# Modulation rows from raw fp32 weights instead of hi and lo halves

## The chip, the cores and the metric

The kernel runs on one core of a Trainium2 chip. The time is that of one execution on the device in microseconds; the figure compared is the median of several runs. The core has a matrix engine (TensorE, PE in the profile; its weight loads are PEld), a vector engine (VectorE, DVE), a scalar engine (ScalarE, ACT), GpSimd (POOL) and SyncE (SP), which here issues the transfers of weights.

## What is computed

The reference is a chain of two networks. The first has two layers whose norms are modulated by a condition vector; the second has two layers without it. The modulation is what matters here: the condition goes through silu and one wide matrix product, and gives shifts, scales and gates for the norms of both layers.

```
def modulate(x, shift, scale):
    return rms_norm(x) * (1.0 + scale) + shift
```

There are two condition vectors of 1024 numbers, for context and latent tokens. For two layers, six chunks and 1024 numbers each that makes 12288 outputs per condition from a 1024 x 12288 weight: 48 tiles of 1 MB, each giving 256 outputs.

## The kernel before, in words

All weights come as 436 tiles of 128 partitions x 2048 fp32 numbers through a ring of four buffers called raw. SyncE issues tile n+4 once TensorE has used tile n. For each tile ScalarE casts raw to fp32r (w_hi, two buffers, `split_hi`, L911), VectorE subtracts to get the rest (w_lo, written over raw, `split_lo`, L1178), and TensorE multiplies with both. A tile is thus a chain of landing, cast, subtraction, matmuls, and its w_hi buffer is free for the tile after next once the matmuls are done.

The order of the work is written out by hand for each engine, with counting semaphores: raw_full (landed), hi_done, lo_done, tile_used, sums_taken (the result was copied out of PSUM).

The first 48 tiles are the modulation. Per tile:
- `ada_rows`: 16 matmuls on TensorE, 8 blocks of 128 input numbers, each with w_hi (L476) and w_lo (L477) as the moving operand of 256 columns, and four stationary columns (the hi and lo parts of two conditions, tile cond). They give 4 x 256 in PSUM.
- `ada_copy` on VectorE (L1264) copies that to ada_row.
- `ada_turn`, one tile later, on TensorE (L484): two small fp32 matmuls put the 256 outputs on partitions, and add hi and lo parts by the 4 x 2 table parts_sum.
- `ada_add` on VectorE (L1268) adds the bias and writes mod.

Beside this ScalarE and GpSimd make tables of decays (L999, L330, L332). After the 48 tiles VectorE adds 1 to the scales (L1286), and the norm begins: ScalarE squares X (L937, after loading a table), TensorE sums the squares by fp32 matmuls of 512 columns with a table of ones (L465), and the product of the first stage (L366 to L368) follows. It needs tiles 48 and 49 split.

Of the kernel before, what the change touches and what calls it, by code (L numbers as in the profile page):

```python
# [26 lines left out]
F32R = mybir.dt.float32r  # L27
ALU = mybir.AluOpType
ACT = mybir.ActivationFunctionType
AX = mybir.AxisListType.X  # L30

P = 128
D = 1024
DC = D // P
T = 256
# [4 lines left out]
RET_H, RET_VB = 4, 4  # L40
# [6 lines left out]
RAW, SPLIT = 4, 2  # L47


ADA_TILES = 48  # L50
# [33 lines left out]
def build(nc, ws, xt, col1, row1, col2, row2, relb, cst, ret_cst, ret_dist, c64, out):  # L84
# [3 lines left out]
    def at(name, shape, kb, dtype=F32):  # L88
        return nc.alloc_sbuf_tensor_at(name, shape, dtype, offset=base + int(kb * KB) // 32 * 32)


    raw = at("raw", [P, RAW, 16, P], 0)
    w_lo = at("w_lo", [P, RAW, 16, P], 0, F32R)
    w_hi = at("w_hi", [P, SPLIT, 16, P], 32, F32R)
# [10 lines left out]
    ident, ones, ones64, rot_ret, rot_diff, swap64 = (cs[:, i, :] for i in range(6))  # L105
    rope_d = at("rope_d", [P, 2, T], 99)
    mod = at("mod", [P, 2, 48, 2], 101)
    cols1 = at("cols1", [P, NCOL1], 101.8)
    cols2 = at("cols2", [P, NCOL2], 102.4)
    silu_c = at("silu_c", [P, DC, 2], 103.1)  # L110
    parts_sum = at("parts_sum", [4, 2], 103.16)
    eps_col = at("eps_col", [P, 2], 103.44)
    lgam = at("lgam", [P, 8], 103.2)
    lam = at("lam", [P, 4], 103.3)
    small = at("small", [P, 16], 103.4)
    softx = at("softx", [P, 2, 16], 103.5)
    rr = at("rr", [P, TT], 104)
    ada_row = at("ada_row", [4, 2, T], 104)
    AR = 106
    cond4 = at("cond4", [P, DC, 4], AR, F32R)  # L120
    SQ = at("SQ", [P, DC, TT], AR)

    QK = at("QK", [P, 16, TT], AR)
# [3 lines left out]
    dist = at("dist", [P, 4, 4, T], AR + 32)  # L127
    expd = at("expd", [P, 2, 4, T], AR + 48)
# [81 lines left out]
    with ExitStack() as ctx:  # L210
        ps = ctx.enter_context(nc.psum_tensor("ps", [P, 8, 512], F32))
# [33 lines left out]
            "inv_done", "inv_next", "rhs_ready", "uw_ready", "uw_taken", "sc_w", "sc_v", "sc_s", "sc_next",  # L245
            "go_sq", "go_sum", "go_var", "go_std", "out_done"))

        waits_passed, ada_turned, cond_ready, cols_in, tables_ready, consts_in = map(sem, ("waits_passed", "ada_turned", "cond_ready", "cols_in", "tables_ready", "consts_in"))
        go_copied, block_ready = map(sem, ("go_copied", "block_ready"))
        (kc_in, za_in, conv_qk, conv_v, ba_in, ba_twice, gates_ready, k_taken, v_turned, v_taken) = map(sem, (  # L250
            "kc_in", "za_in", "conv_qk", "conv_v", "ba_in", "ba_twice", "gates_ready", "k_taken", "v_turned",
# [8 lines left out]
        def tiles(phase, layer, eng, body, first=0, count=None, per=4):  # L260


            n0, _, total = PH[phase]
            count = total - first if count is None else count
            turns = count // per
            done = 0
            if turns > 1:
                with eng.Fori(0, turns) as i:
                    for u in range(per):
                        body(i, u, n0 + first + u, i * (per // 4) + layer * (NL // 4))  # L270
                done = turns * per
            for u in range(done, count):
                body(0, u, n0 + first + u, layer * (NL // 4))
# [12 lines left out]
        def raw_slot(s):  # L286
            return s % RAW
# [69 lines left out]
        def _(pe):  # L357
# [18 lines left out]
            def wait_tile(s, turn):  # L376
                pe.wait_ge(lo_done, turn * 4 + s + 1)
# [89 lines left out]

            pe.sem_inc(tile_used, SPLIT)

            def ada_rows(i, u, s, turn):  # L470

                wait_tile(s, turn)
                pe.wait_ge(sums_taken, i * 4 + s + 1)
                o = ps[0:4, 4 + u % 2, 0:T].rearrange("p (a b) -> p a b", b=P)
                for c in range(DC):
                    mm(o, cond4[:, c, :], w_hi[:, s % SPLIT, c:16:DC, :], start=c == 0, stop=False)  # L476
                    ins = mm(o, cond4[:, c, :], w_lo[:, raw_slot(s), c:16:DC, :], start=False, stop=c == DC - 1)  # L477
                ins.then_inc(tile_used, 1)

            def ada_turn(t, u):  # L480

                pe.wait_ge(sums_taken, t + 3)
                for mi in range(2):
                    ins = mm(ps[:, 6 + u % 2, 2 * mi:2 * mi + 2], ada_row[:, u % 2, mi * P:mi * P + P],  # L484
                             parts_sum[:], start=True, stop=True)
                ins.then_inc(ada_turned, 1)

            pe.wait_ge(cond_ready, 1)

            def first_tiles(i, u, s, turn):  # L490
                ada_rows(i, u, s, turn)
                if u == 1:
                    pe.wait_ge(tables_ready, 1)
                if u:
                    ada_turn(u - 1, u - 1)

            def later_tiles(i, u, s, turn):
                ada_rows(i, u, s, turn)
                ada_turn(i * 4 + s - 1, (u - 1) % 4)
            tiles("ada", 0, pe, first_tiles, 0, 4)  # L500
            tiles("ada", 0, pe, later_tiles, 4)
            ada_turn(ADA_TILES - 1, 3)
            pe.wait_ge(consts_in, 16)
            pe.wait_ge(mod_ready, ADA_TILES)

# [398 lines left out]
        def _(act):  # L904
            fn = nc.scalar.activation

            def split_hi(s, turn):

                act.wait_ge(raw_full[raw_slot(s)], turn * 16 + 16 * (s // 4 + 1))
                act.wait_ge(tile_used, turn * 4 + s + 1)  # L910
                nc.scalar.copy(w_hi[:, s % SPLIT], raw[:, raw_slot(s)]).then_inc(hi_done, 1)  # L911

            def only_split(phase, layer, first=0, count=None, per=4):
                tiles(phase, layer, act, lambda i, u, s, turn: split_hi(s + SPLIT, turn), first, count, per)
# [48 lines left out]
            def swiglu(phase, layer, dst, width, number):  # L963
# [13 lines left out]
            act.wait_ge(cols_in, 16)  # L977
            fn(silu_c[:], cols1[:, C_COND:C_COND + 16].rearrange("p (a b) -> p a b", b=2), ACT.Silu
               ).then_inc(silu_c_ready, 1)
            split_hi(0, 0)  # L980
            split_hi(1, 0)

            act.wait_ge(lgam_abs, 1)
            fn(small[:, 0:8], small[:, 0:8], ACT.Exp).then_inc(lgam_exp, 1)
            act.wait_ge(lgam_one, 1)
            fn(small[:, 8:16], rr[:, 0:8], ACT.Ln).then_inc(lgam_ln, 1)

            def ada_decays(i, u, s, turn):

                split_hi(s + SPLIT, turn)  # L990
                h = u // 3
                if u == 2:
                    act.wait_ge(lgam_ready, 1)
                    act.wait_ge(dist_in, 16)
                if u % 3 == 2:
                    if h:
                        act.wait_ge(decays_ready, h)
                    for d in range(2):
                        fn(expd[:, d], dist[:, d], ACT.Exp, scale=lgam[:, 4 * d + h:4 * d + h + 1]  # L999
                           ).then_inc(decays_exp, 1)  # L1000
            tiles("ada", 0, act, ada_decays, 0, 3 * RET_H, per=3 * RET_H)
            only_split("ada", 0, 3 * RET_H)
            act.wait_ge(x_in, 16)
            act.wait_ge(mod_scaled, 1)
            norm(0, slice(0, TT), ada_gains(0, 0, both), h_hi)
# [165 lines left out]
        def _(dve):  # L1171
# [3 lines left out]
            def split_lo(s, turn):  # L1175

                dve.wait_ge(hi_done, turn * 4 + s + 1)
                tt(w_lo[:, raw_slot(s)], raw[:, raw_slot(s)], w_hi[:, s % SPLIT].bitcast(F32), ALU.subtract  # L1178
                   ).then_inc(lo_done, 1)

            def each(phase, layer, take, first=0, count=None, per=4, split_first=False):

                def body(i, u, s, turn):
                    if split_first:
                        split_lo(s + SPLIT, turn)
                    dve.wait_ge(tile_used, turn * 4 + s + 1 + SPLIT)
                    take(i, u)
                    if not split_first:
                        split_lo(s + SPLIT, turn)
                tiles(phase, layer, dve, body, first, count, per)  # L1190

            def halves(hi, lo, src):

                copy(hi, src)
                dve.drain()
                return tt(lo, src, hi.bitcast(F32), ALU.subtract)
# [39 lines left out]
            nc.vector.memset(small[:], 0.0)  # L1236
            nc.vector.memset(eps_col[:, 0:1], EPS)
            nc.vector.memset(eps_col[:, 1:2], LN_EPS)
            dve.drain()
            dve.wait_ge(silu_c_ready, 1)  # L1240
            halves(cond4[:, :, 0:2], cond4[:, :, 2:4], silu_c[:]).then_inc(cond_ready, 1)
            split_lo(0, 0)
            split_lo(1, 0)
            dve.wait_ge(logit_in, 16)
            stt(small[:, 0:8], lgam[:], -1.0, lgam[:], ALU.mult, ALU.min).then_inc(lgam_abs, 1)
            dve.wait_ge(lgam_exp, 1)
# [10 lines left out]
            dve.drain()  # L1257
            stt(lgam[:], lgam[:], 0.0, small[:, 8:16], ALU.min, ALU.subtract).then_inc(lgam_ready, 1)

            dve.wait_ge(consts_in, 16)  # L1260
            tt(parts_sum[:], ident[0:4, 0:2], ident[0:4, 2:4], ALU.add).then_inc(tables_ready, 1)

            def ada_copy(u):
                copy(ada_row[:, u % 2], ps[0:4, 4 + u % 2, 0:T]).then_inc(sums_taken, 1)  # L1264

            def ada_add(t, u):
                dve.wait_ge(ada_turned, t + 1)
                tt(mod[:].rearrange("p l c v -> p (l c) v")[:, bass.ds(t * 2, 2), :],  # L1268
                   ps[:, 6 + u % 2, 0:4].rearrange("p (a b) -> p a b", b=2),
                   cols1[:, bass.ds(t * 2, 2)].unsqueeze(2).to_broadcast([P, 2, 2]), ALU.add).then_inc(mod_ready, 1)  # L1270

            def first_ada(i, u):
                ada_copy(u)
                if u:
                    ada_add(u - 1, u - 1)

            def later_ada(i, u):
                ada_copy(u)
                ada_add(i * 4 + u + 3, (u - 1) % 4)
            each("ada", 0, first_ada, 0, 4)  # L1280
            each("ada", 0, later_ada, 4)
            ada_add(ADA_TILES - 1, 3)
            dve.drain()
            for l in range(2):
                for w in (1, 4):
# [744 lines left out]
```

## Time and profile before

| | us |
|---|---|
| runs | 3595.68, 3597.95, 3603.71 |
| median | 3597.95 |
| profiled execution | 3598.84 |
| its span | 3597.1 |
| PE busy (x22972) | 3284.3 |
| DVE busy | 1857.5 |
| ACT busy | 1336.3 |

The page of the profile gives busy times over the whole span. A record of a matmul lasts from the start of its reading to a modelled end, so records overlap, and the pace is the distance between two starts, not a record's length. An fp32 matmul leaves two records, an fp32r one leaves one. The modulation takes the first 197 us of the span, so the rows below are read from that stretch.

### The profile page before, as it was taken

How to read it: one execution, taken by the hardware profiler on the slowest of the kernel's cores; microseconds unless marked ns; L12 is line 12 of the kernel's file. 1: busy time of each engine (PE TensorE's matmuls, PEld its weight loads, DVE VectorE, ACT ScalarE, POOL GpSimd, SP SyncE). 2: the span in 40 equal slices, each digit the busy share in tenths (PEclk: the TensorE clock that was granted, in tenths of full speed). 3: DMA queues.
4: the chain of work that ended last, by engine and by line, in shares of the span. 5: the costliest groups of instructions: out<-in, count | busy, mean ns of one | idle time of the engine just before them, and what ended most of it. 6: DMA issues, size and time to landing. Idle time of an engine off the chain costs nothing.

```text
span 3597.1 us, 56408 instructions
## 1 busy us (share of the span) xinstructions
PE 3284.3 (91%) x22972; PEld 2948.3 (82%) x22972; DVE 1857.5 (52%) x2346; ACT 1336.3 (37%) x1355; POOL 59.9 (2%) x36
## 2 busy tenths in 40 slices
PE   6889889989997966999999999899999999998998
PEld 4559657868786935999998887799999988878997
DVE  6843434333323375545544774655465457745554
ACT  5541112142213144434534451454354334414443
POOL 4000000000000000001000000000000000000000
PEclk7999999999998988999999898999999999989999
DMA  7832102212222201545544421354545533213553
GB/s 282 319 113 94 47 0 82 94 71 93 99 88 72 106 12 47 175 165 191 180 183 143 150 98 56 117 184 178 187 159 185 182 145 133 103 71 121 184 183 132
DMA packets 65619, 469.85 MB, mean 131 GB/s; under 512 B 7296, under 2 KB 8480, under 8 KB 9152
## 3 DMA queue, kind: packets, MB, share of 16 engines
q1 hardware_dynamic: 64112, 460.42, 35.5%
q0 software_dynamic: 1360, 7.33, 0.6%
q8 instruction: 110, 1.80, 0.2%
q14 instruction: 37, 0.30, 0.0%
HBM read 466.67 MB, written 1.05 MB: 130 GB/s over the span
## 4 chain that ended last, share of the span: by engine, by line
PE 86%; DVE 6%; ACT 3%; DVEq 2%; issue 2%; ACTq 1%; DMA 1%; SPq 0%
PE ps L366 23%; PE ps L367 22%; PE ps L368 22%; DVE w_lo L1178 2%; PE ps L374 2%; PE ps L373 2%; PE ps L372 2%; PE ps L465 2%; ACT w_hi L911 1%; PE ps L476 1%; PE ps L477 1%; PE ps L536 1%; ACTq L948 1%; PE ps L737 1%; PE ps L461 1%
## 5 line engine op out<-in xcount | busy, mean ns | idle before, releaser
L1178 DVE TENSOR_TENSOR w_lo<-raw,w_hi 128x2048 fp32r<-128x2048 f32 x436 | 1015.7, 2330 | 846.3 <-ACT w_hi L911 845.4
L911 ACT CAST w_hi<-raw 128x2048 fp32r<-128x2048 f32 x436 | 830.4, 1905 | 1558.4 <-PE ps L368 1315.7
L366 PE MATMUL ps<-l_hi,w_hi 128*128 128x256 f32 x2896 | 841.8, 291 | 31.9 <-DVE l_lo L1215 23.1
L367 PE MATMUL ps<-l_lo,w_hi 128*128 128x256 f32 x2896 | 828.8, 286 | 0.0
L368 PE MATMUL ps<-l_hi,w_lo 128*128 128x256 f32 x2896 | 828.5, 286 | 0.0
L366 PEld LDWEIGHTS ps<-l_hi,w_hi 128*128 128x128 f32 x2896 | 564.6, 195 | 48.4 <-issue 45.9
L367 PEld LDWEIGHTS ps<-l_lo,w_hi 128*128 128x128 f32 x2896 | 565.8, 195 | 0.4
L368 PEld LDWEIGHTS ps<-l_hi,w_lo 128*128 128x128 f32 x2896 | 565.2, 195 | 0.0
L366 PE MATMUL ps<-h_hi,w_hi 128*128 128x512 f32 (+1 forms) x1088 | 387.1, 356 | 32.3 <-DVE h_lo L1215 32.3
L367 PE MATMUL ps<-h_lo,w_hi 128*128 128x512 f32 (+1 forms) x1088 | 384.3, 353 | 0.0
L368 PE MATMUL ps<-h_hi,w_lo 128*128 128x512 f32 (+1 forms) x1088 | 384.2, 353 | 0.0
L366 PE MATMUL ps<-fh_hi,w_hi 128*128 128x256 f32 x1024 | 290.2, 283 | 0.0
L367 PE MATMUL ps<-fh_lo,w_hi 128*128 128x256 f32 x1024 | 289.8, 283 | 0.0
L368 PE MATMUL ps<-fh_hi,w_lo 128*128 128x256 f32 x1024 | 289.8, 283 | 0.0
L366 PEld LDWEIGHTS ps<-h_hi,w_hi 128*128 128x128 f32 x1088 | 210.2, 193 | 66.4 <-issue 40.1
L367 PEld LDWEIGHTS ps<-h_lo,w_hi 128*128 128x128 f32 x1088 | 210.6, 194 | 26.7 <-issue 0.2
L368 PEld LDWEIGHTS ps<-h_hi,w_lo 128*128 128x128 f32 x1088 | 210.5, 193 | 26.6
L366 PEld LDWEIGHTS ps<-fh_hi,w_hi 128*128 128x128 f32 x1024 | 196.6, 192 | 0.6
L367 PEld LDWEIGHTS ps<-fh_lo,w_hi 128*128 128x128 f32 x1024 | 196.6, 192 | 0.0
L368 PEld LDWEIGHTS ps<-fh_hi,w_lo 128*128 128x128 f32 x1024 | 196.6, 192 | 0.0
L476 PE MATMUL ps<-w_hi,cond 128*4 128x256 f32 x384 | 107.4, 311 | 49.4 <-DVE w_lo L1178 48.8
L366 PE MATMUL ps<-hid_hi,w_hi 128*128 (+2 forms) x352 | 120.4, 342 | 11.0 <-DVE small L1232 11.0
(380 smaller groups left out, 4563.2 us busy)
## 6 DMA issues: line engine op xcount, KB each, us to landing
raw<-in_ws SPq DMA_DIRECT2D x436, 1024.0 KB, 4.8
dist<-in_ret_dist POOLq DMA_DIRECT2D x1, 2048.0 KB, 13.9
X<-in_xt SPq DMA_DIRECT2D x1, 2048.0 KB, 23.1
relB<-in_relb POOLq DMA_DIRECT2D x2, 1024.0 KB, 5.7
out<-X SPq DMA_DIRECT2D x1, 1024.0 KB, 4.8
rows<-in_row POOLq DMA_DIRECT2D x2, 332.0 KB, 3.2
rope_r<-in_ret_cst POOLq DMA_DIRECT2D x1, 512.0 KB, 17.1
cs<-in_cst POOLq DMA_DIRECT2D x1, 384.0 KB, 7.1
```

Of the source, the lines that this page charges most:

```text
L366: mm(out_, w_hi[:, s % SPLIT, blk], rhs_hi, start=start, stop=False)
L367: mm(out_, w_hi[:, s % SPLIT, blk], rhs_lo, start=False, stop=False)
L368: return mm(out_, w_lo[:, raw_slot(s), blk], rhs_hi, start=False, stop=stop)
L372: mm(out_, x_hi, w_hi[:, s % SPLIT, blk], start=start, stop=False)
L373: mm(out_, x_hi, w_lo[:, raw_slot(s), blk], start=False, stop=False)
L374: return mm(out_, x_lo, w_hi[:, s % SPLIT, blk], start=False, stop=stop)
L461: ins = mm(ps[:, 4, 0:width], ones, X[:, c, cols], start=c == 0, stop=c == DC - 1)
L465: ins = mm(ps[:, 5, 0:width], ones, SQ[:, c, 0:width], start=c == 0, stop=c == DC - 1)
L476: mm(o, cond4[:, c, :], w_hi[:, s % SPLIT, c:16:DC, :], start=c == 0, stop=False)
L477: ins = mm(o, cond4[:, c, :], w_lo[:, raw_slot(s), c:16:DC, :], start=False, stop=c == DC - 1)
L911: nc.scalar.copy(w_hi[:, s % SPLIT], raw[:, raw_slot(s)]).then_inc(hi_done, 1)
L1178: tt(w_lo[:, raw_slot(s)], raw[:, raw_slot(s)], w_hi[:, s % SPLIT].bitcast(F32), ALU.subtract).then_inc(lo_done, 1)
```

## The change

In the modulation TensorE no longer reads w_hi and w_lo: the moving operand is raw, as fp32, and the stationary one is silu_c, the two condition columns in fp32. There are 8 fp32 matmuls a tile in place of 16 in fp32r, the result has 2 rows, and the turn uses a 2 x 2 identity. The 48 casts and 48 subtractions of these tiles go; the counters hi_done and lo_done are raised by 48 at once. The splits of tiles 48 and 49 stay: ScalarE does them after the decay tables, VectorE after the last addition. The loops over tiles are written out, and ScalarE makes the decay tables one after another at the start.

```diff
-                wait_tile(s, turn)
-                pe.wait_ge(sums_taken, i * 4 + s + 1)
-                o = ps[0:4, 4 + u % 2, 0:T].rearrange("p (a b) -> p a b", b=P)
+                pe.wait_ge(raw_full[raw_slot(t)], 16 * (t // RAW + 1))
+                pe.wait_ge(sums_taken, t + 1)
+                o = ps[0:2, 4 + t % 2, 0:T].rearrange("p (a b) -> p a b", b=P)
                 for c in range(DC):
-                    mm(o, cond4[:, c, :], w_hi[:, s % SPLIT, c:16:DC, :], start=c == 0, stop=False)
-                    ins = mm(o, cond4[:, c, :], w_lo[:, raw_slot(s), c:16:DC, :], start=False, stop=c == DC - 1)
+                    ins = mm(o, silu_c[:, c, :], raw[:, raw_slot(t), c:16:DC, :], start=c == 0, stop=c == DC - 1)
                 ins.then_inc(tile_used, 1)
...
-                    ins = mm(ps[:, 6 + u % 2, 2 * mi:2 * mi + 2], ada_row[:, u % 2, mi * P:mi * P + P],
-                             parts_sum[:], start=True, stop=True)
+                    ins = mm(ps[:, 6 + t % 2, 2 * mi:2 * mi + 2], ada_row[:, t % 2, mi * P:mi * P + P],
+                             ident[0:2, 0:2], start=True, stop=True)
...
+            act.sem_inc(hi_done, ADA_TILES)
...
+            for s in range(ADA_TILES, ADA_TILES + SPLIT):
+                act.wait_ge(raw_full[raw_slot(s)], 16 * (s // RAW + 1))
+                nc.scalar.copy(w_hi[:, s % SPLIT], raw[:, raw_slot(s)]).then_inc(hi_done, 1)
...
+            dve.sem_inc(lo_done, ADA_TILES)
...
-            dve.wait_ge(silu_c_ready, 1)
-            halves(cond4[:, :, 0:2], cond4[:, :, 2:4], silu_c[:]).then_inc(cond_ready, 1)
-            split_lo(0, 0)
-            split_lo(1, 0)
...
+            for t in range(ADA_TILES):
+                dve.wait_ge(tile_used, t + 1 + SPLIT)
+                ada_copy(t)
+                if t:
+                    ada_add(t - 1)
+            ada_add(ADA_TILES - 1)
+            for s in range(ADA_TILES, ADA_TILES + SPLIT):
+                split_lo(s, 0)
```

On VectorE, at the end of the modulation, the order before was (the last tile of the loop, what follows it, and the norm):

```order
L1264 COPY ada_row<-ps 4x256
L1268 ISA
L1268 TENSOR_TENSOR mod<-ps,cols_64 128x4
L1178 TENSOR_TENSOR w_lo<-raw,w_hi 128x2048
L268 REGISTER_ALU
L268 COMPARE_AND_BRANCH
L1268 TENSOR_TENSOR mod<-ps,cols_64 128x4
L1286 TENSOR_SCALAR mod<-mod 128x16 x4
L1211 TENSOR_TENSOR SQ<-X,rr 128x512 x8
```

And in the changed kernel, the same place (L1243 is the copy, L1247 the addition, L1163 the subtraction, L1262 the scaling):

```order
L1243 COPY ada_row<-ps 2x256
L1247 TENSOR_TENSOR mod<-ps,cols_64 128x4
L1243 COPY ada_row<-ps 2x256
L1247 TENSOR_TENSOR mod<-ps,cols_64 128x4 x2
L1163 TENSOR_TENSOR w_lo<-raw,w_hi 128x2048 x2
L1262 TENSOR_SCALAR mod<-mod 128x16 x4
L1196 TENSOR_TENSOR SQ<-X,rr 128x512 x8
```

The two subtractions of tiles 48 and 49 moved from behind the last two copies to a place between the last addition and the scaling.

On TensorE each tile of the modulation is now eight row matmuls and the two of the turn:

```order
L474 MATMUL ps<-raw,silu_c 2x256 x16
L483 MATMUL ps<-cs,ada_row 128x2 x2
L474 MATMUL ps<-raw,silu_c 2x256 x8
L483 MATMUL ps<-cs,ada_row 128x2 x2
L474 MATMUL ps<-raw,silu_c 2x256 x8
```

Before, sixteen matmuls (L476 and L477 in turn) stood in the place of each eight.

## Rows read from the trace of the kernel before

**Rows 1.** The page: the span.
```profile
span 3597.1 us, 56408 instructions
```
**Rows 2.** Stretches: bounds, length, busy (records) per engine, granted clock, DMA share, GB/s.
```profile
40.00:95.00 55.00, 44.34 (x237) 27.82 (x238) 47.02 (x38) 27.30 (x18) 31.39 (x7) 0.69 0.61 221
95.00:192.00 97.00, 78.31 (x618) 55.11 (x619) 80.93 (x93) 58.93 (x31) 0.00 (x0) 1.00 0.88 326
```
**Rows 3.** Waits, 95 to 192 us: total us, times, longest.
```profile
ACT w_hi L911 <- PE ps L477: 40.4, 31, 2.5
PEld ps L476 <- DVE w_lo L1178: 21.3, 30, 1.3
```
**Rows 4.** VectorE in order of time: start, us, instruction, idle time before.
```profile
143.91 2.29 DVE L1178 TENSOR_TENSOR w_lo<-raw,w_hi 128x2048 fp32r<-128x2048 f32 x1
...
150.21 2.29 DVE L1178 TENSOR_TENSOR w_lo<-raw,w_hi 128x2048 fp32r<-128x2048 f32 x1
```
**Rows 5.** fp32 matmuls: TensorE in order of time, a record's lengths, the norm's stretch.
```profile
437.69 1.89 PE L536 MATMUL ps<-att,V 128*128 128x256 f32 x8
1923.59 3.72 PE L461 MATMUL ps<-X,cs 128*128 128x256 f32 x16 [0.92 <-DVE X L1492]
L536 PE MATMUL ps<-att,V x128: 379/379/634, 432.5 to 536.1; 128*128 128x256 f32 x128
1923.60:1927.30 3.70, 3.70 (x16) 2.94 (x16) 2.29 (x1) 2.29 (x2) 0.00 (x0) 1.00 0.79 283
199.50:204.40 4.90, 4.90 (x6) 2.12 (x7) 0.00 (x0) 3.45 (x7) 0.00 (x0) 0.50 0.00 0
```
**Rows 6.** TensorE at full clock, end of a tile's rows and turn.
```profile
141.55 0.28 PE L476 MATMUL ps<-w_hi,cond 128*4 128x256 f32 x1
141.66 0.28 PE L477 MATMUL ps<-w_lo,cond 128*4 128x256 f32 x1
141.87 0.60 PE L484 MATMUL ps<-parts_sum,ada_row 4*128 4x2 f32 x4
...
141.86 0.52 PEld L484 LDWEIGHTS ps<-parts_sum,ada_row 4*128 4x128 f32 x4 [0.23 <-issue]
```
**Rows 7.** The same at half clock.
```profile
44.72 0.41 PE L477 MATMUL ps<-w_lo,cond 128*4 128x256 f32 x1
45.07 0.92 PEld L484 LDWEIGHTS ps<-parts_sum,ada_row 4*128 4x128 f32 x4 [0.43 <-issue]
46.01 0.38 PE L476 MATMUL ps<-w_hi,cond 128*4 128x256 f32 x1
```
**Rows 8.** ScalarE's casts that a landing released, and transfers at the start.
```profile
6.85 1.90 ACT L911 CAST w_hi<-raw 128x2048 fp32r<-128x2048 f32 x1 [3.74 <-DMA raw<-in_ws]
11.97 1.90 ACT L911 CAST w_hi<-raw 128x2048 fp32r<-128x2048 f32 x1 [3.22 <-DMA raw<-in_ws]
21.80 1.91 ACT L911 CAST w_hi<-raw 128x2048 fp32r<-128x2048 f32 x1 [1.90 <-DMA raw<-in_ws]
29.33 1.90 ACT L911 CAST w_hi<-raw 128x2048 fp32r<-128x2048 f32 x1 [5.62 <-DMA raw<-in_ws]
3.70 0.50 SPq L308 DMA_DIRECT2D X<-in_xt  x1
X<-in_xt SPq DMA_DIRECT2D x1, 2048.0 KB, 23.1
```
**Rows 9.** Stretches as in rows 2.
```profile
23.60:37.00 13.40, 9.95 (x46) 5.92 (x44) 5.81 (x7) 7.27 (x6) 2.19 (x1) 0.50 0.91 379
```
**Rows 10.** End of the modulation, in order of time.
```profile
194.01 0.40 DVE L1264 COPY ada_row<-ps 4x256 f32<-4x256 f32 x1
194.44 2.29 DVE L1178 TENSOR_TENSOR w_lo<-raw,w_hi 128x2048 fp32r<-128x2048 f32 x1
197.39 1.28 ACT L918 ACT_TABLE_LOAD   x1 [2.98 <-DVE mod L1286]
199.46 9.63 PE L465 MATMUL ps<-SQ,cs 128*128 128x512 f32 x16 [4.38 <-ACT SQ L937]
```

More of the change, by code:

```diff
@@ L110, in build @@
     silu_c = at("silu_c", [P, DC, 2], 103.1)
-    parts_sum = at("parts_sum", [4, 2], 103.16)
     eps_col = at("eps_col", [P, 2], 103.44)
@@ L117, in build @@
     rr = at("rr", [P, TT], 104)
-    ada_row = at("ada_row", [4, 2, T], 104)
+    ada_row = at("ada_row", [2, 2, T], 104)
     AR = 106
-    cond4 = at("cond4", [P, DC, 4], AR, F32R)
     SQ = at("SQ", [P, DC, TT], AR)
@@ L246, in build @@
             "go_sq", "go_sum", "go_var", "go_std", "out_done"))
-        waits_passed, ada_turned, cond_ready, cols_in, tables_ready, consts_in = map(sem, ("waits_passed", "ada_turned", "cond_ready", "cols_in", "tables_ready", "consts_in"))
+        waits_passed, ada_turned, cols_in, consts_in = map(sem, ("waits_passed", "ada_turned", "cols_in", "consts_in"))
         go_copied, block_ready = map(sem, ("go_copied", "block_ready"))
@@ L468, in _, with ada_rows, ada_turn @@
             pe.sem_inc(tile_used, SPLIT)
-            def ada_rows(i, u, s, turn):
-                wait_tile(s, turn)
-                pe.wait_ge(sums_taken, i * 4 + s + 1)
-                o = ps[0:4, 4 + u % 2, 0:T].rearrange("p (a b) -> p a b", b=P)
+            def ada_rows(t):
+                pe.wait_ge(raw_full[raw_slot(t)], 16 * (t // RAW + 1))
+                pe.wait_ge(sums_taken, t + 1)
+                o = ps[0:2, 4 + t % 2, 0:T].rearrange("p (a b) -> p a b", b=P)
                 for c in range(DC):
-                    mm(o, cond4[:, c, :], w_hi[:, s % SPLIT, c:16:DC, :], start=c == 0, stop=False)
-                    ins = mm(o, cond4[:, c, :], w_lo[:, raw_slot(s), c:16:DC, :], start=False, stop=c == DC - 1)
+                    ins = mm(o, silu_c[:, c, :], raw[:, raw_slot(t), c:16:DC, :], start=c == 0, stop=c == DC - 1)
                 ins.then_inc(tile_used, 1)
-            def ada_turn(t, u):
+            def ada_turn(t):
                 pe.wait_ge(sums_taken, t + 3)
+                if t >= 2:
+                    pe.wait_ge(mod_ready, t - 1)
                 for mi in range(2):
-                    ins = mm(ps[:, 6 + u % 2, 2 * mi:2 * mi + 2], ada_row[:, u % 2, mi * P:mi * P + P],
-                             parts_sum[:], start=True, stop=True)
+                    ins = mm(ps[:, 6 + t % 2, 2 * mi:2 * mi + 2], ada_row[:, t % 2, mi * P:mi * P + P],
+                             ident[0:2, 0:2], start=True, stop=True)
                 ins.then_inc(ada_turned, 1)
[L488 to L502, printed above, removed]
+            pe.wait_ge(silu_c_ready, 1)
+            for t in range(ADA_TILES):
+                ada_rows(t)
+                if t == 1:
+                    pe.wait_ge(consts_in, 16)
+                if t:
+                    ada_turn(t - 1)
+            ada_turn(ADA_TILES - 1)
             pe.wait_ge(consts_in, 16)
@@ L979, in _ @@
                ).then_inc(silu_c_ready, 1)
-            split_hi(0, 0)
-            split_hi(1, 0)
+            act.sem_inc(hi_done, ADA_TILES)
             act.wait_ge(lgam_abs, 1)
@@ L986, in _ @@
             fn(small[:, 8:16], rr[:, 0:8], ACT.Ln).then_inc(lgam_ln, 1)
[L988 to L1002, printed above, removed]
+            act.wait_ge(lgam_ready, 1)
+            act.wait_ge(dist_in, 16)
+            for h in range(RET_H):
+                if h:
+                    act.wait_ge(decays_ready, h)
+                for d in range(2):
+                    fn(expd[:, d], dist[:, d], ACT.Exp, scale=lgam[:, 4 * d + h:4 * d + h + 1]).then_inc(decays_exp, 1)
+            for s in range(ADA_TILES, ADA_TILES + SPLIT):
+                act.wait_ge(raw_full[raw_slot(s)], 16 * (s // RAW + 1))
+                nc.scalar.copy(w_hi[:, s % SPLIT], raw[:, raw_slot(s)]).then_inc(hi_done, 1)
             act.wait_ge(x_in, 16)
@@ L1258, in _, with ada_copy, ada_add @@
             stt(lgam[:], lgam[:], 0.0, small[:, 8:16], ALU.min, ALU.subtract).then_inc(lgam_ready, 1)
[L1260 to L1266, printed above, removed]
-                dve.wait_ge(ada_turned, t + 1)
[L1268 to L1282, printed above, removed]
+            def ada_copy(t):
+                copy(ada_row[:, t % 2], ps[0:2, 4 + t % 2, 0:T]).then_inc(sums_taken, 1)
+            def ada_add(t):
+                dve.wait_ge(ada_turned, t + 1)
+                tt(mod[:].rearrange("p l c v -> p (l c) v")[:, 2 * t:2 * t + 2, :],
+                   ps[:, 6 + t % 2, 0:4].rearrange("p (a b) -> p a b", b=2),
+                   cols1[:, 2 * t:2 * t + 2].unsqueeze(2).to_broadcast([P, 2, 2]), ALU.add).then_inc(mod_ready, 1)
+            dve.wait_ge(cols_in, 16)
+            for t in range(ADA_TILES):
+                dve.wait_ge(tile_used, t + 1 + SPLIT)
+                ada_copy(t)
+                if t:
+                    ada_add(t - 1)
+            ada_add(ADA_TILES - 1)
+            for s in range(ADA_TILES, ADA_TILES + SPLIT):
+                split_lo(s, 0)
             dve.drain()
```

## The prediction

> **What bounds the kernel now.** The page comes first. The profiled execution took 3598.84 us, its span 3597.1 [rows 1], so 1.7 us lie around the span, and it stands 0.9 us above the median of the runs (3597.95). The change touches only the modulation, the first 48 of 436 weight tiles, so I read the stretches of that part, then its waits, then its instructions in order of time, and last the instructions behind it.
>
> From 95 to 192 us TensorE has its full clock and is busy 78.3 of 97 us, VectorE 80.9, and the DMA engines move 326 GB/s [rows 2]. Nothing is saturated: the waits show a ring. ScalarE waits for TensorE to give back one of the two w_hi buffers (40.4 us in all), TensorE for VectorE's w_lo (21.3 and more) [rows 3]. In order of time the ring is seen as a subtraction every 6.30 us for each second tile (143.91, 150.21), that is 3.15 us a tile [rows 4]. From 40 to 95 us GpSimd is busy too and the clock is 0.69 [rows 2]; the tiles take longer there.
>
> **The tile's price on TensorE.** Removed are 16 fp32r matmuls a tile, added are 8 fp32 ones over the same 256 columns, with two stationary columns in place of four. The trace of before has no fp32 matmul with so few stationary columns. It has them with 128: each appears as two records. Eight records of L536 end 1.89 us after the first began; less one record's own 0.379 us, over seven steps, that is 0.216 us from one to the next. Sixteen records of L461, in a stretch at the full clock, give (3.72 - 0.379)/15 = 0.223 us [rows 5]. At the half clock the norm's records with 512 columns pass at about 0.85 us, six in 4.9 us [rows 5]; for 256 columns that is 0.427. The step is then 256 columns twice per record at the clock granted, and an fp32r record of before steps 0.11 us at the full clock [rows 6], once its columns.
>
> Bounds for the unknown: below, a record with two stationary columns could pass like an fp32r one (0.11); above, it steps 0.223. I take 0.216, nearest to rows of the same moving width, so 16 x 0.216 = 3.46 us for a tile's rows (1.76 to 3.57).
>
> The Trainium skill, "FP8 and Floating Point Precision", TensorE Precision Notes, has true fp32 as four passes through the array, whatever the stationary width. That is a rule against this change: by it the eight matmuls stream 8 x 4 x 256 columns where the sixteen of before streamed 16 x 256, and 8192 columns at 2.4 GHz are an estimated 3.41 us, against the 3.46 that rows of another stationary width give; the low bound is out by it, and the sum would be 2 us less.
>
> To this comes the turning of the rows, two small fp32 matmuls (four records), which stays. At the full clock the last row record starts at 141.66, its successor would at 141.77, the turn starts at 141.87, and its loads take 0.52 [rows 6]; at the half clock the next tile starts 0.02 behind such loads' end (45.07 + 0.92 against 46.01) [rows 7]. So 0.10 + 0.52 + 0.02 = 0.64 us; one of 2 stationary rows has the same 128 columns to load. A tile costs 3.46 + 0.64 = 4.10; I take 4.12 us, with a little of the 0.223 (4.04 to 4.21). At the half clock it is 16 x 0.427 + (46.01 - 44.72 - 0.21) = 7.91 us [rows 7].
>
> So TensorE takes the place of the ring as what bounds the stage, at 4.12 where 3.15 was from 95 us on. ScalarE's 48 casts (1.90 us) and VectorE's 48 subtractions leave, and with them the ring and what GpSimd's work adds to it; that lets the stretch up to 95 us run as fast as the rest, but no faster than TensorE; the transfers are covered: the queue of raw tiles delivers one in 2.5 us (below).
>
> **When it starts.** Now TensorE waits for raw itself. ScalarE's casts that a landing ended began at 6.85, 11.97, 21.80 and 29.33 us: tiles 0, 1, 3 and 4 [rows 8]. X, issued at 3.70 between tiles 3 and 4, takes 23.1 us to land, 26.8 [rows 8], and tile 4 lands 2.5 us behind it: the queue delivers in order, and GpSimd's tables take their part of the rate early on. An earlier issue of tile 4 (its buffer is free after tile 0, which TensorE ends between 10.3 and 13.8) changes nothing. Tiles 0 to 3 at 4.12 or even 7.91 us: tile 1 from 12, tile 2 from 17, tile 3 from 21.8 to 25.9 (29.7 at the half clock). Both end about when tile 4 lands, 29.3. From there on a tile is delivered in 2.5 us and eaten in 4.12, and the buffers fill.
>
> Last row record of tile 47: 29.4 + 43 x 4.12 + 3.46 = 210.0 us.
>
> **The clock.** Before, it was at half from 23.6 to 37 us [rows 9] and 0.69 in the mean from there to 95 [rows 2], while TensorE had waits in each tile. Here it stands idle 1 us ahead of tiles 2 and 3 and 3 us ahead of tile 4, so a half stretch at tile 4 is likely; one of 3 to 7 us costs half its length. I add 1.5 us (0 to 6). Afterwards TensorE has no pause but the 0.1 us ahead of each turn, and the full clock lasted from 95 to 192 us with 78.3 of 97 us busy [rows 2]. End of the rows: 211.5.
>
> **Behind it.** VectorE's order changed. Before, the subtractions of tiles 48 and 49, which the next product needs, stood ahead of the last two additions; only the last (2.29) was behind the last copy [rows 10]. Now both stand between the last addition and the scaling of mod, for which ScalarE's norm waits. From the end of the rows: copy 0.45, turn 0.65, addition 0.2, two subtractions 4.5, drain and scaling 0.6 (0.66 from the end of the last subtraction to the table load before, the last addition among it): 6.4 to 6.5 us, so ScalarE's table load starts at 218.1, against 197.39 before [rows 10]. That is +20.7, of which 2.2 us are the reordering. Behind this the stages are unchanged. The norm's matmuls took 9.63 us, half of it at the half clock [rows 5, 10]; a longer idle time ahead (7 us instead of 4.4) may put more of them at the half clock, fewer by luck: -2 to +4, taken as 0. The decay tables, now made earlier on ScalarE and GpSimd, lie off the path. The removed split of the condition lay ahead of TensorE's first work, which now waits for DMA.
>
> **Sum.** 3598.84 + 20.7 = 3619.5 as the profiled execution goes, less 0.9 as the median: 3619 us, +0.58%. Errors: 43 tiles x (-0.08 to +0.09) = -3.4 to +3.9; clock early -1.5 to +4.5; norm -2 to +4. Together 3612 to 3630.
>
> **The rivals.**
> (1) The full clock isn't held under fp32 matmuls with two stationary columns. For: it wasn't held from 40 to 95 us (0.69), with four columns. Against: there TensorE had waits, and from 95 us on it was held at four columns; the fp32 records of L461 ran at 1.00 [rows 5]. With the granted clock of 0.69, 38% of the time at 4.12 and 62% at 7.91 a tile, a tile takes 5.86: 44 x 1.74 = +77 on the forecast, 3696; wholly at half, 3786.
> (2) The other side: a record with two stationary columns passes in one go. A tile is then 1.76 + 0.64 = 2.40 on TensorE, less than the delivery of 2.5, which becomes the bound; rows end at 29.3 + 44 x 2.5 = 139.3 and the table load starts at 145.8: 51.6 us less than before, 3546. It decides from a step under 0.157 us per record (3.15 - 0.64 over 16); for it speaks only that no row shows such a width, against it that 512 and 256 columns scale with the moving side alone.
> (3) The turn hides behind the rows' stream, its loads pulled ahead. Then a tile is 3.46 and the sum 43 x 0.66 = 28 less: 3591, a little faster; with part of it hidden, no change. Against: the idle time ahead of the turn's loads and the start of the next tile only after them, at both clocks [rows 6, 7].
> (4) The change is paid but hidden elsewhere, in that the weight stream of the stages behind gains from fuller buffers. Against: the norm stands in between, and raw, w_hi and w_lo are full there before as well. Nothing to price.
>
> **Chances.** The forecast 0.86 (3612 to 3630); (1) 0.06, (2) 0.03, (3) 0.05, half of it within 0.2%, half faster. A run can be told from no change from about 0.2% (7 us). Slower 0.91, same 0.04, faster 0.05. The range is 3611 to 3634, with the near part of (1), short stretches at the half clock: 0.84 of the chance.
>
> **What would show it.** In the profile of after: 768 records of the rows' line (two per matmul) stepping 0.216 us at clock 1.00; a tile each 4.1 us from about 30 to 211 us; TensorE over 95% busy there; DMA near 250 GB/s; no wait of TensorE on raw after tile 4; the last rows near 210 and the table load near 218 us; both subtractions between the last addition and the scaling. The forecast is wrong if the step is 0.11 or half-clock stretches come back after 40 us.

## The result and the profile after

| | before | after |
|---|---|---|
| median, us | 3601.02 (5 runs) | 3614.45 (5 runs, 3613.28 to 3620.00) |
| ratio, 95% interval | | 1.0044 (1.0029 to 1.0058) |
| ratio, second series | | 1.0049 (1.0035 to 1.0063) |
| span of the profiled execution | 3597.1 | 3611.5 |
| norm's table load starts | 197.39 | 216.02 |

The change makes the kernel 0.4 to 0.5% slower. The forecast was 3619 us; the range of 3611 to 3634 holds the median. The forecast started from a median of 3597.95 us before; in the five runs compared here it is 3601.02, so the medians differ by 13.4 us and the ratios give 15.8 and 17.6, where about 21 were forecast.

The page of the changed kernel: span, busy time, the group of the row matmuls with its waits.

```profile
span 3611.5 us, 56037 instructions
PE 3335.3 (92%) x22972; PEld 2937.5 (81%) x22972; DVE 1739.2 (48%) x2295; ACT 1243.8 (34%) x1307; POOL 51.3 (1%) x36
L474 PE MATMUL ps<-raw,silu_c 128*2 128x256 f32 x768 | 177.8, 386 | 10.5 <-DMA raw<-in_ws 10.5
```

VectorE has 118 us less to do and ScalarE 93 us less, and the span is 14.4 us longer: work was taken from engines that had time, and TensorE, which sets the end, got more. The stretches say it in the columns of [rows 2]:

```profile
40.00:95.00 55.00, 55.00 (x272) 24.06 (x270) 7.46 (x26) 2.19 (x2) 12.63 (x4) 1.00 0.72 261
95.00:192.00 97.00, 97.00 (x478) 42.68 (x477) 13.77 (x48) 0.00 (x0) 0.00 (x0) 1.00 0.72 256
29.50:32.90 3.40, 3.40 (x10) 1.02 (x8) 0.00 (x0) 0.09 (x1) 3.23 (x1) 0.50 1.01 422
```

TensorE has records without a gap in both stretches, at the full clock, and the transfers fall from 326 to 256 GB/s, since nobody asks for more. The third row is the only piece of the stage at the half clock from tile 4 on. (The first two tiles, from 6.68 to 16.55 us, begin with records 0.43 us apart, the pace of the half clock; tile 2 lands only at 17.8, so nearly nothing comes of it.) In order of time TensorE shows the start, the tile that waits for its landing, and the steady pace:

```profile
17.80 3.62 PE L474 MATMUL ps<-raw,silu_c 128*2 128x256 f32 x16 [0.72 <-DMA raw<-in_ws]
29.14 5.30 PE L474 MATMUL ps<-raw,silu_c 128*2 128x256 f32 x16 [3.11 <-DMA raw<-in_ws]
34.37 0.60 PE L483 MATMUL ps<-cs,ada_row 2*128 2x2 f32 x4
34.90 3.62 PE L474 MATMUL ps<-raw,silu_c 128*2 128x256 f32 x16
38.45 0.60 PE L483 MATMUL ps<-cs,ada_row 2*128 2x2 f32 x4
38.98 3.62 PE L474 MATMUL ps<-raw,silu_c 128*2 128x256 f32 x16
```

From 34.90 to 38.98 is a tile, 4.08 us; sixteen records are (3.62 - 0.379)/15 = 0.216 us apart. Tile 4 begins at 29.14, where [rows 8] have its landing at 29.33. The end of the stage, answering to [rows 10]:

```profile
209.67 1.18 PE L483 MATMUL ps<-cs,ada_row 2*128 2x2 f32 x8
209.77 0.41 DVE L1243 COPY ada_row<-ps 2x256 f32<-2x256 f32 x1 [3.38 <-PE ps L474]
210.88 0.16 DVE L1247 TENSOR_TENSOR mod<-ps,cols 128x4 f32<-128x4 f32 x1 [0.41 <-PE ps L483]
210.96 4.48 DVE L1163 TENSOR_TENSOR w_lo<-raw,w_hi 128x2048 fp32r<-128x2048 f32 x2
215.54 0.41 DVE L1262 TENSOR_SCALAR mod<-mod 128x16 f32<-128x16 f32 x4
216.02 1.28 ACT L910 ACT_TABLE_LOAD   x1 [7.19 <-DVE mod L1262]
218.09 10.05 PE L463 MATMUL ps<-SQ,cs 128*128 128x512 f32 x16 [7.25 <-ACT SQ L929]
```

Both subtractions stand between the last addition and the scaling, and ScalarE waits 7.19 us for it, where it waited 2.98.

### The profile page after: what moved, and what is told of

Its sections match the earlier page's. It is cut to its first block, busy times and chain, and to the rows that moved or that the text cites. A ratio compares the mean times of both kernels' runs of the same rounds, so it can differ in the third digit from the quotient of the medians.

```text
span 3611.5 us, 56037 instructions
## 1 busy us (share of the span) xinstructions
PE 3335.3 (92%) x22972; PEld 2937.5 (81%) x22972; DVE 1739.2 (48%) x2295; ACT 1243.8 (34%) x1307; POOL 51.3 (1%) x36
## 4 chain that ended last, share of the span: by engine, by line
PE 88%; DVE 4%; ACT 3%; DVEq 2%; issue 1%; ACTq 1%; DMA 1%; SPq 0%
PE ps L364 23%; PE ps L365 22%; PE ps L366 22%; PE ps L474 5%; PE ps L463 2%; PE ps L371 2%; PE ps L372 2%; PE ps L370 2%; ACTq L940 1%; PE ps L528 1%; ACT w_hi L903 1%; PE ps L729 1%; PE ps L483 1%; PE ps L459 1%; DMA raw<-in_ws 1%
## 5 line engine op out<-in xcount | busy, mean ns | idle before, releaser
L1163 DVE TENSOR_TENSOR w_lo<-raw,w_hi 128x2048 fp32r<-128x2048 f32 x388 | 890.0, 2294 | 807.8 <-ACT w_hi L903 807.4
L903 ACT CAST w_hi<-raw 128x2048 fp32r<-128x2048 f32 x386 | 734.5, 1903 | 1475.8 <-PE ps L366 1315.6
L474 PE MATMUL ps<-raw,silu_c 128*2 128x256 f32 x768 | 177.8, 386 | 10.5 <-DMA raw<-in_ws 10.5
L474 PEld LDWEIGHTS ps<-raw,silu_c 128*2 128x2 f32 x768 | 62.2, 86 | 103.2 <-issue 13.3
```

The lines of the kernel that those rows point to most:

```text
L474: ins = mm(o, silu_c[:, c, :], raw[:, raw_slot(t), c:16:DC, :], start=c == 0, stop=c == DC - 1)
```

## The experiments

Table load is the start of ScalarE's table load ahead of the first norm, that is the end of the modulation; ratios are to the kernel before in the runs of the same chip.

| kernel | median us (runs) | ratio, interval | table load | span |
|---|---|---|---|---|
| turn twice | 3638.46 (2) | 1.0108 (1.0088 to 1.0128) | 237.86 | 3636.0 |
| half of the rows | 3551.37 (2) | 0.9866 (0.9846 to 0.9886) | 149.10 | 3550.3 |
| 128 stationary columns | 3623.54 (2) | 1.0066 (1.0043 to 1.0089) | 219.26 | 3617.3 |
| subtractions aside, first | 3614.89 (6) | 1.0039 (1.0025 to 1.0052) | 211.81 | 3613.9 |
| subtractions aside, second | 3613.33 (5) | 1.0035 (1.0021 to 1.0049) | 211.73 | 3610.7 |
| changed kernel again | 3616.31 (5) | 1.0049 (1.0035 to 1.0063) | 216.01 | 3614.6 |
| first 16 tiles raw | 3589.72 (9) | 0.9974 (0.9964 to 0.9984) | 186.30 | 3587.1 |
| every second raw | 3579.25 (5) | 0.9949 (0.9936 to 0.9963) | 181.49 | 3577.3 |
| every third raw | 3609.91 (7) | 1.0030 (1.0019 to 1.0041) | 208.66 | 3611.8 |
| every third, one at a time | 3599.84 (10) | 1.0000 (0.9991 to 1.0009) | 194.39 | 3598.5 |
| second, then third | 3575.83 (5) | 0.9929 (0.9915 to 0.9942) | 178.16 | 3574.7 |

**Is the turn in series?** Its two matmuls run twice.

```diff
-                for mi in range(2):
+                for mi in (0, 1, 0, 1):
```

> The changed kernel, with the two small matmuls of each turn run twice. Theory (TensorE bounds the stage and the turn is in series with the rows): each tile costs 0.52 to 0.54 us more, a pace of 4.61 in place of 4.08; 48 turns give +25 us on the table load (241), and the time near 3640. Rival (the turn hides behind the rows' stream): less than 5 us more.

```profile
104.08 1.05 PE L483 MATMUL ps<-cs,ada_row 2*128 2x2 f32 x8
105.06 3.62 PE L474 MATMUL ps<-raw,silu_c 128*2 128x256 f32 x16
108.61 1.05 PE L483 MATMUL ps<-cs,ada_row 2*128 2x2 f32 x8
```

The pace is 4.53 us a tile, 0.45 more, where 0.52 to 0.54 were expected, and the table load is 21.8 us later (48 x 0.45 = 21.6), at 237.86 in place of 241. The turn is in series, as forecast. A second turn costs four more steps of its loads (0.45) and not the whole 0.52 of a group, which contains the end of the last load once. The rival of a hidden turn falls.

**What is next below the fp32 passes?** Four of the eight row matmuls left out, so half of the modulation's sums is missing.

```diff
-                for c in range(DC):
-                    ins = mm(o, silu_c[:, c, :], raw[:, raw_slot(t), c:16:DC, :], start=c == 0, stop=c == DC - 1)
+                for c in range(0, DC, 2):
+                    ins = mm(o, silu_c[:, c, :], raw[:, raw_slot(t), c:16:DC, :], start=c == 0, stop=c == DC - 2)
```

> The changed kernel with four of the eight fp32 row matmuls of each tile left out (half of the modulation's sums is missing). TensorE then needs 1.74 + 0.61 = 2.35 us a tile. Theory (TensorE's fp32 passes bound the stage, and the landings of one raw tile in 2.5 us come next): pace 2.5 a tile, table load at 29.1 + 44 x 2.5 + 7 = 146 us, time 3545. If the four buffers' turnaround is next rather than the rate (4.8 us from issue to landing, plus use), the pace is still below 3 us, 3565 at most. Rival (the pace comes from the queue of weights already, and TensorE only looks busy): the table load stays near 216.

TensorE in order of time, then a stretch of the steady part:

```profile
104.58 1.89 PE L474 MATMUL ps<-raw,silu_c 128*2 128x256 f32 x8
106.40 0.60 PE L483 MATMUL ps<-cs,ada_row 2*128 2x2 f32 x4
107.05 1.89 PE L474 MATMUL ps<-raw,silu_c 128*2 128x256 f32 x8
60.00:140.00 80.00, 77.17 (x386) 35.51 (x384) 18.39 (x64) 0.00 (x0) 0.00 (x0) 1.00 1.01 422
```

Now the DMA engines are full (share 1.01, 422 GB/s) and a tile takes 2.47 to 2.49 us; the table load came at 149.10 (146 expected). TensorE is close behind with 77.17 of 80 us. So the stage's three prices are: landings 2.5, the ring of before 3.15, fp32 on TensorE 4.08. The change went from the second to the third. The time of this kernel, 66.9 us less at the table load than the changed one, is also what the fp32 passes cost beyond the transfers. That a stationary operand of two columns would pass cheaper, the rival on the fast side, had already fallen with the 0.216 us of the changed kernel.

**Does the stationary width matter?** The table of ones, 128 columns, in place of the two conditions; the modulation is then another one.

```diff
-                o = ps[0:2, 4 + t % 2, 0:T].rearrange("p (a b) -> p a b", b=P)
+                if t == 0:
+                    pe.wait_ge(consts_in, 16)
+                o = ps[:, 4 + t % 2, 0:T].rearrange("p (a b) -> p a b", b=P)
...
-                    ins = mm(o, silu_c[:, c, :], raw[:, raw_slot(t), c:16:DC, :], start=c == 0, stop=c == DC - 1)
+                    ins = mm(o, ones, raw[:, raw_slot(t), c:16:DC, :], start=c == 0, stop=c == DC - 1)
```

> The changed kernel with 128 stationary columns (the table of ones) in the fp32 row matmuls in place of the two condition columns, so the modulation isn't the reference's. Theory (a record's step is twice its moving columns, whatever the stationary width): step 0.213 to 0.216 us, pace 4.08 to 4.15 a tile, time within 0.1% of the changed kernel. Rival (narrow stationary operands are cheaper, wide ones are limited by their loads): step 0.22 or more and a pace of 4.2 or more, +5 us or more.

```profile
104.15 0.60 PE L485 MATMUL ps<-cs,ada_row 2*128 2x2 f32 x4
104.68 3.72 PE L476 MATMUL ps<-raw,cs 128*128 128x256 f32 x16
108.33 0.60 PE L485 MATMUL ps<-cs,ada_row 2*128 2x2 f32 x4
```

The tile is 4.18, 0.10 more than 4.08. Sixteen records take 3.72 us, the length of L461's sixteen in [rows 5], but a mean step of 0.223 is not how they run. The first two records of such a run show it, here, in L461's run of before, and in the changed kernel:

```profile
104.68 0.70 PE L476 MATMUL ps<-raw,cs 128*128 128x256 f32 x2
1923.59 0.70 PE L461 MATMUL ps<-X,cs 128*128 128x256 f32 x2 [0.92 <-DVE X L1492]
34.90 0.59 PE L474 MATMUL ps<-raw,silu_c 128*2 128x256 f32 x2
```

With 128 stationary columns the second record starts 0.70 - 0.379 = 0.32 us behind the first, with two 0.21. After it the step is (3.72 - 0.70)/14 = 0.216 us in both. So the theory held for the step: it is 0.216 whatever the stationary width, and 128 columns cost 0.10 us once, at the head of each tile's run. The eight records of L536 in [rows 5], which run on from others, step 0.216 with 128 columns too. The pace of 4.18 lies a little above the 4.15 that the theory allowed, and the rival's +5 us didn't come: the table load is 3.2 us later, since tile 4, ahead of which TensorE stood idle 1.67 us here and 3.11 in the changed kernel, ran at the full clock (3.72 us against 5.30).

The prediction named four passes from the Trainium skill ("FP8 and Floating Point Precision", TensorE Precision Notes). The trace agrees: an fp32 matmul takes two records, 0.43 us, where one in fp32r steps 0.11 [rows 6]. The page gives the passes without a word on the stationary width; that the width hardly matters is what this run shows.

**Are the two subtractions on the path?** The one of tile 48 behind the copy of tile 46, the one of tile 49 behind the scaling.

```diff
+                if t == ADA_TILES - 2:
+                    split_lo(ADA_TILES, 0)
             ada_add(ADA_TILES - 1)
-            for s in range(ADA_TILES, ADA_TILES + SPLIT):
-                split_lo(s, 0)
...
             ins.then_inc(mod_scaled, 1)
+            split_lo(ADA_TILES + 1, 0)
```

> The changed kernel, with VectorE's subtraction of tile 48 behind the copy of tile 46 and that of tile 49 behind the scaling of mod. Theory (both subtractions stand on the path between the last addition and the norm): the norm's table load comes 4.5 us earlier than in the changed kernel (216.0), at 211.5, and the time is 4 to 5 us less, about 3610. Rival (the reordering is hidden, the norm waits for something else such as X or the clock): the table load moves, but the sums of squares end where they did, no change. Product of tile 49 could wait for its subtraction instead: then part of it comes back at the first product.

```profile
211.06 0.16 DVE L1247 TENSOR_TENSOR mod<-ps,cols 128x4 f32<-128x4 f32 x1 [0.41 <-PE ps L483]
211.32 0.41 DVE L1262 TENSOR_SCALAR mod<-mod 128x16 f32<-128x16 f32 x4
211.64 2.29 DVE L1163 TENSOR_TENSOR w_lo<-raw,w_hi 128x2048 fp32r<-128x2048 f32 x1
211.81 1.28 ACT L910 ACT_TABLE_LOAD   x1 [2.97 <-DVE mod L1262]
```

The table load came 4.21 us earlier, and the end of the norm's sums (ScalarE's next instruction behind the squares) at 222.71 in place of 228.18; the other 1.3 us are the clock, for the norm's matmuls took 8.80 us in place of 10.05. Behind the norm TensorE's product waits for h_lo (8.8 us) and, in this profile, not for the subtraction of tile 49, so nothing is given back there. Yet the first median was that of the changed kernel. So the pair was run again on one chip.

> The changed kernel once more, unchanged, beside the runs of the other three. The norm's table load is at 216 +- 2 us again, since the stage in front of it is paced by TensorE alone; the part behind it, which differed by 8 us between profiles (3368.5 to 3376.9 from the first norm's sum to the last's), moves by its half-clock stretches and not by the change. Median 3612 to 3618.

> The changed kernel with the subtractions beside the path, once more. Theory (both on the path, scatter behind it hid the gain the first time): the table load at 211.8 again, and a median 3 to 5 us under that of the changed kernel on the same chip. Rival (the gain is given back behind the first norm in every execution): medians within 1 us of each other although the table load is 4.2 us earlier.

Table loads at 216.01 and 211.73, medians 3616.31 and 3613.33. The medians lie 3.0 us apart in the forecast direction, but the intervals of the ratios (1.0035 to 1.0063, 1.0021 to 1.0049) overlap. Both series together, ten runs against eleven, give 3616.0 and 3613.5. In the trace the 4.2 us are shown twice; in the whole time they are likely and not proven, for the part behind scatters as much: from the first norm's sum to the last's it took 3373.4 us before, 3368.5 after, 3371.8 in the second profile of the same kernel, 3376.4 and 3373.2 in the two of this one.

**Can the two ways be mixed?** The changed kernel pays TensorE and spares ScalarE and VectorE; before, it is the reverse. Three mixes of raw and split tiles follow. The first makes the decay tables at the start, as the changed kernel does, the others spread over the first casts, behind every second one. The tiles that are raw in each of the three:

```diff
+    RAW_TILES = [t for t in range(ADA_TILES) if t < 16]
+    RAW_TILES = [t for t in range(ADA_TILES) if t % 2 == 0]
+    RAW_TILES = [t for t in range(ADA_TILES) if t % 3 == 0]
```

A split tile keeps the four-column cond and a 4 x 256 result, a raw one has two; the subtraction of tile t+2 follows the addition behind tile t, except in the third mix, where those of t+2 and t+3 follow each third tile. That of tile 49 is behind the scaling in all.

> Tiles 0 to 15 as in the changed kernel (raw fp32), tiles 16 to 47 as before (hi and lo parts); decay tables as in the changed kernel, subtraction of tile 49 behind the scaling. Theory (raw fp32 wins where GpSimd's work and the early ring slow the split tiles, and loses where the ring runs at 3.15): 12 tiles at 4.08 from 29.2 us end at 78, 32 at 3.15 end at 179, table load at 184 to 186 in place of 197.4 before; time 12 us less than before, about 3588. Rival (the split tiles' ring needs more than 3.15 after the switch, or the clock falls when TensorE gets its waits back): table load at 197 or later, no gain.

> Every second tile raw fp32 (even ones), the others split in hi and lo. Theory (TensorE bounds: 4.08 for a raw tile and 1.87 + 0.61 = 2.48 for a split one, 6.56 a pair; ScalarE and VectorE have one tile to split in that time and their ring is loose): 3.28 a tile, 44 tiles end at 173.5, table load at 176; time 21 us less than before, about 3579. Rival (a split tile's chain of cast and subtraction, 4.3 us, isn't covered by its raw neighbour because its landing comes late): waits of TensorE on the subtraction, pace 3.6 or more, 3593 or more.

> Every third tile raw fp32 (0, 3, ...), the two between split. Theory: TensorE needs 4.08 + 2 x 2.48 = 9.04 us for three, 3.01 a tile, and the ring of two w_hi buffers 6.3 for two, so 44 tiles end at 162 and the table load is at 165; time 32 us less than before, about 3568. Rival (with subtractions of 4 us beside GpSimd's work, and raw tiles that land 4.8 us behind their issue, the cover is too short): TensorE waits for w_lo in each group, pace 3.2 to 3.4 and the table load at 175 to 182.

The first two came near what was expected: table loads 186.30 (184 to 186) and 181.49 (176), 0.26% and 0.51% less time than before. The second mix, TensorE's turns of two pairs, then 30 to 95 us:

```profile
31.04 0.60 PE L499 MATMUL ps<-parts_sum,ada_row 4*128 4x2 f32 x4
33.53 0.60 PE L499 MATMUL ps<-cs,ada_row 2*128 2x2 f32 x4
37.61 0.60 PE L499 MATMUL ps<-parts_sum,ada_row 4*128 4x2 f32 x4
30.00:95.00 65.00, 64.15 (x394) 35.04 (x392) 34.85 (x50) 25.30 (x16) 30.45 (x8) 1.00 0.81 308
```

A pair takes 6.57 us against 6.56 forecast. Its table load is 5.5 us late because of the start, not of the pace: tile 1, the first split one, waited 7.4 us for its subtraction, and the clock was then at half (0.51 from 16 to 30 us). The third mix missed: its table load is 44 us later than expected, and its median 3609.91 in place of 3568. VectorE in order of time in the third mix, and TensorE's waits in the stage (total, times, longest):

```profile
61.45 8.79 DVE L1286 TENSOR_TENSOR w_lo<-raw,w_hi 128x2048 fp32r<-128x2048 f32 x2
70.17 0.41 DVE L1281 COPY ada_row<-ps 2x256 f32<-2x256 f32 x1
```
```profile
PEld ps L499 <- DVE ada_row L1281: 27.4, 10, 6.6
PE ps L499 <- DVE ada_row L1281: 24.5, 10, 6.3
```

Two subtractions together, the second beside GpSimd's work, hold VectorE for 8.79 us, and the copy that the turn needs stands behind them. Two repairs were tried: one subtraction at a time, and with this order every second tile raw until tile 19, then every third.

```diff
-            LO_AT = {**{-1: [1], 0: [2]}, **{t: [t + 2, t + 3] for t in range(1, ADA_TILES) if t % 3 == 2 and t + 3 < ADA_TILES}}
+            LO_AT = {**{t - 2: [t] for t in SPLIT_TILES if t > 1}, **({-1: [1]} if 1 in SPLIT_TILES else {})}
...
-    RAW_TILES = [t for t in range(ADA_TILES) if t % 3 == 0]
+    RAW_TILES = [t for t in range(ADA_TILES) if (t % 2 == 0 if t < 20 else t % 3 == 2)]
```

(The last two lines are in the second repair alone, which also makes the tables one cast earlier.)

> Every third tile raw as in the third mix, but VectorE subtracts for one tile at a time, two tiles ahead, in place of two subtractions together. Theory (the two together kept VectorE from copying the rows out, and TensorE's turn waited for that copy, 24.5 us in the third mix): those waits go, the table load moves from 208.7 to 180 to 188, and the time is 20 us less than the third mix, 3582 to 3590. Rival (what held the third mix is the late landing of raw tiles, and the half clock up to 93 us): the table load stays above 200.

> Every second tile raw up to tile 19, as in the second mix, then every third; subtractions two tiles ahead. Theory: up to tile 19 as the second mix (3.28 a tile, at about 97 us with its late start), then 9.04 us for three tiles in place of 9.84: 28 tiles save 7.5 us, table load at 174 in place of 181.5, time 3572. Rival (split tiles two in a row wait for landing, cast and subtraction): pace 3.2 or more, no gain over the second mix, 3577 to 3582.

One at a time took 14.3 us off the third mix, not 20 or more: its table load at 194.39 lies between what theory and rival gave, and its median is 3599.84 where 3582 to 3590 were expected, about that of before (3598.73). From 30 to 95 us TensorE still has gaps, from 95 us on few:

```profile
30.00:95.00 65.00, 51.51 (x300) 29.11 (x299) 38.64 (x41) 29.65 (x20) 38.34 (x8) 0.87 0.67 251
95.00:170.00 75.00, 70.23 (x471) 41.78 (x468) 47.26 (x63) 28.51 (x15) 0.00 (x0) 1.00 0.84 325
```

TensorE waits for w_lo, 27.5 us in all: 7.9 ahead of tile 1, 13.5 from 30 to 95 us, where two subtractions in three tiles are too many while GpSimd works, and 6.1 later. The last kernel uses just that, and is the fastest of all: 3575.83 us, ratio 0.9929 (0.9915 to 0.9942), 23 us less than before. Its interval overlaps that of the second mix, but each of its five runs is shorter than each of the other's five, and before took the same on both chips (3598.73 and 3598.80). In it TensorE is busy 62.64 of 65 us and 73.12 of 75 us in the same two stretches; in the second one three tiles take 9.1 us where TensorE doesn't wait (9.04 forecast) and 9.3 in the mean, and the table load is at 178.16, 4 us later than I expected.

**Where the mixes gain.** Each tile's rows are copied out once, so the copies up to 95 us count the tiles. Before, the second mix and the last kernel, in VectorE's copies alone:

```profile
0.00:95.00 95.00, 6.60 (x17) 0.75 0.72 278
0.00:95.00 95.00, 9.05 (x22) 0.93 0.85 331
0.00:95.00 95.00, 8.62 (x21) 0.93 0.83 325
```

The second mix is 5 tiles ahead at 95 us, which at some 3.2 us each is the whole 15.9 us by which its table load is earlier. Behind 95 us it is not faster than before: 3.28 us a tile against 3.15. Only the thirds of the last kernel (3.1) are a little faster there. Even the changed kernel is 2 tiles ahead at 95 us (19 copies), and loses behind it. So the mixes gain above all while GpSimd works, most likely because they take subtractions from VectorE there (busy 34.85 of 65 us from 30 to 95 us in the second mix, 53.15 before). A kernel with all tiles split and GpSimd's tables made elsewhere might gain as much; no run tests that.

## Why the prediction was right

The forecast was right in direction and in mechanism, and a few us too long. Step by step, as it had it:

- *TensorE takes the place of the ring.* Right: no wait of TensorE on raw after tile 4, and the stage shortens by 67 us when half of its fp32 rows go.
- *A row record steps 0.216, not 0.11 and not 0.223.* Measured 0.216, with two columns. The choice was right, but the 0.223 was a misreading: no record steps so, it is 0.216 with 0.10 us once at the head of a run, spread over fifteen steps. The tile at 4.12 was 0.04 too long: 0.02 is the turn, 0.02 the "little of the 0.223" that I added without ground. Over 43 tiles (4.12 against 4.077 in the mean) it makes 1.9 us, nearly all of the 2.1 us by which the table load came earlier than the 218.1 forecast.
- *Turn 0.64 in series.* Measured as 4.08 - 3.46 = 0.62; doubled, it costs 0.45 more.
- *Start set by landings, tile 4 at 29.3.* 29.14.
- *Clock +1.5.* From tile 4 on one half-clock stretch, on that tile (5.30 us against 3.62): +1.7. Then the full clock to the end of the stage, with 0.98 as the mean from 30 to 95 us in three of the four profiles of the changed order. The rival of a clock not held falls. The size hung on little: with 128 stationary columns, where TensorE stood idle 1.67 us ahead of tile 4 in place of 3.11, that tile met no half-clock stretch at all.
- *Tail 6.4 to 6.5, of it 2.2 for the reordering.* From the last row record's end (about 209.6) to 216.02 it is 6.4; the forecast's sum had room for 6.6 (211.5 to 218.1). But putting both subtractions aside gives 4.2 us, since in the kernel before one was on the path as well (the second in [rows 10]).
- *Norm unchanged.* 10.05 against 9.63.

What the sum missed is behind the norm. The table load was 18.6 us later, the span 14.4 longer. The forecast took that part as unchanged; in the two profiles it differs by 4.9 us from the first norm's sum to the last's, 3.0 of it before the second norm, in the heads of the retention. There before and after run the same eight matmuls of a sum of squares in 5.40 and 3.70 us:

```profile
448.87 5.40 PE L545 MATMUL ps<-sqh,cs 128*128 128x512 f32 x8 [2.21 <-ACT sqh L1011]
448.00:456.00 8.00, 6.35 (x12) 2.84 (x13) 2.65 (x5) 3.34 (x6) 0.00 (x0) 0.79 0.00 0
```
```profile
468.29 3.70 PE L537 MATMUL ps<-sqh,cs 128*128 128x512 f32 x8 [2.21 <-ACT sqh L996]
467.00:475.00 8.00, 5.92 (x18) 3.43 (x19) 3.96 (x6) 3.69 (x6) 0.00 (x0) 1.00 0.00 0
```

The difference is the granted clock (0.79 and 1.00), after the same 2.21 us of waiting. Over the thirteen profiles this part took 3368.5 to 3377.4 us, with no order by what was changed in front; the profile of after has the shortest. In the second profile of the changed kernel it was 3371.8, and its span 17.5 us over that of before. The ratios give 15.8 and 17.6 us, against 20.7 forecast from the profiles; of the gap of 3.1 to 4.9 us 2.1 are the stage. The rest is of the size of that scatter, and I did not find an effect of the change in it; that is argued from thirteen profiles, not shown by a run that fixes the clock.

## What to carry to other kernels

Price a removed split by the engine that gets the work. Here an fp32 matmul with 256 moving columns took two records of 0.216 us, about four times the 0.11 of one in fp32r, with 2 stationary columns as with 128. So 8 fp32 matmuls in place of 16 in fp32r took about twice the streaming time, and freeing ScalarE and VectorE bought nothing from 95 us on, where TensorE had more to do than the ring took. Where two ways of one step load different engines, a mix can beat both: half and then a third of the tiles raw was 0.7% faster than all split and 1.1% faster than all raw. Look where such a gain arises: here most of it lies in the stretch in which GpSimd slows VectorE. And place the long instruction of the shared engine one at a time: two together cost 14 us of the table load. A mean taken over a run of records hides what happens once at its head; look at the first two by themselves.

## What was not expected of the hardware

GpSimd and VectorE hinder each other both ways. GpSimd's addition of the decay tables, by line of before and of after:

```profile
L332 POOL TENSOR_TENSOR DM<-expd x4: 3800/4254/4257, 39.9 to 81.1; 128x1024 f32<-128x1024 f32 x4
```
```profile
L330 POOL TENSOR_TENSOR DM<-expd x4: 2337/2339/2341, 25.0 to 52.9; 128x1024 f32<-128x1024 f32 x4
```

It takes 2.34 us where VectorE only copies, and 4.25 beside the subtractions. Of the subtractions of before, the twelve in that stretch:

```profile
L1178 DVE TENSOR_TENSOR w_lo<-raw,w_hi x12: 2268/4056/4951, 36.6 to 87.8; 128x2048 fp32r<-128x2048 f32 x12
```

A subtraction takes 2.29 us outside that stretch and 4.06 in the median within it.
